# The residual scaled ahead of eight accumulating transfers, and one set of weights split earlier, in a one-core transformer layer

## The reference, cut to what matters

```
x = layer_norm(ALPHA * x + mixed, ln1_g, ln1_b)
h = square(relu(x @ w_up))                     # 512 x 4096
x = layer_norm(ALPHA * x + h @ w_down, ln2_g, ln2_b)
```

## Time and profile before

| | |
|---|---|
| three executions | 833.61, 830.8, 833.26 us; median 833.26 |
| the profiled execution | 841.54 us, its span 839.7 us, mean granted clock 0.984 |
| PE busy | 804.4 us, 96% of the span |
| DVE busy | 551.4 us, 66% |
| ACT busy | 403.2 us, 48% |
| POOL busy | 117.9 us, 14% |
| DMA | 168.45 MB, mean 201 GB/s |

### The profile page before, as it was taken

One profiled execution on the slowest core, in us unless ns is written; L12 is line 12 of the kernel. 1 busy time (PEld: TensorE's weight loads), 2 busy tenths in 40 slices (PEclk: granted clock), 3 DMA queues, 4 the chain that ended last, 5 costly groups with the idle time before them and its releaser, 6 DMA issues.

```text
span 839.7 us, 11669 instructions
## 1 busy us (share of the span) xinstructions
PE 804.4 (96%) x4779; PEld 714.0 (85%) x4779; DVE 551.4 (66%) x587; ACT 403.2 (48%) x457; POOL 117.9 (14%) x123
## 2 busy tenths in 40 slices
PE   9999999999999999999999999909999999999995
PEld 8889888898888889989988898807998899889974
DVE  4656556665569338686685777609568946974798
ACT  5658334583236225434461237601467357635843
POOL 1211111421111111111011111121012000000006
PEclk9999999999999999999999999968999999999999
DMA  9696776768676987956987497868999955555522
GB/s 312 222 306 214 188 143 145 175 125 164 202 260 165 261 176 138 310 75 171 350 281 172 59 260 190 178 109 262 280 256 265 252 202 182 172 201 198 201 101 100
DMA packets 81251, 168.45 MB, mean 201 GB/s; under 512 B 3341, under 2 KB 33078, under 8 KB 77622
## 3 DMA queue, kind: packets, MB, share of 16 engines
q1 hardware_dynamic: 58358, 109.08, 37.8%
q0 software_dynamic: 22848, 58.73, 34.4%
HBM read 165.70 MB, written 60.82 MB: 270 GB/s over the span
## 4 chain that ended last, share of the span: by engine, by line
issue 54%; PE 30%; POOL 10%; DVE 4%; DMA 1%; ACT 0%; SPq 0%; DVEq 0%; POOLq 0%
PE bank L1949 10%; PE bank L1950 10%; PE bank L1951 10%; POOL kept L697 7%; POOL kept L687 2%; DVE two L1786 1%; DVE w_lo L1221 1%; POOL y_lo L704 1%; DMA two<-in_mem_dram 1%; DVE y_lo L1221 0%; PE bank L1976 0%; POOL two L734 0%; DVE decay L1792 0%; DVE smx L1792 0%; POOL y_hi L702 0%
## 5 line engine op out<-in xcount | busy, mean ns | idle before, releaser
L1949 PE MATMUL bank<-x_hi,w_hi 128*128 128x512 f32 (+1 forms) x624 | 211.8, 339 | 0.0
L1950 PE MATMUL bank<-x_lo,w_hi 128*128 128x512 f32 (+1 forms) x624 | 210.6, 338 | 0.0
L1951 PE MATMUL bank<-x_hi,w_lo 128*128 128x512 f32 (+1 forms) x624 | 210.6, 338 | 0.0
L1949 PE MATMUL bank<-w_hi,y_hi 128*128 128x512 f32 x304 | 120.1, 395 | 25.7 <-DVE two L1786 22.7
L1221 DVE TENSOR_TENSOR w_lo<-raw,w_hi 128x2048 fp32r<-128x2048 f32 (+2 forms) x52 | 111.2, 2140 | 37.8 <-ACT w_hi L1050 28.7
L1949 PEld LDWEIGHTS bank<-x_hi,w_hi 128*128 128x128 f32 x624 | 118.4, 190 | 12.7 <-issue 0.3
L1951 PEld LDWEIGHTS bank<-x_hi,w_lo 128*128 128x128 f32 x624 | 118.4, 190 | 12.5
L1950 PEld LDWEIGHTS bank<-x_lo,w_hi 128*128 128x128 f32 x624 | 118.4, 190 | 12.2
L1951 PE MATMUL bank<-w_hi,y_lo 128*128 128x512 f32 x304 | 119.3, 392 | 0.0
L1950 PE MATMUL bank<-w_lo,y_hi 128*128 128x512 f32 x304 | 119.3, 392 | 0.0
L697 POOL DMA_DIRECT2D kept<-kept x56 | 64.6, 1153 | 361.3 <-issue 331.4
(11 more groups left out here) (269 smaller groups left out, 1388.1 us busy)
## 6 DMA issues: line engine op xcount, KB each, us to landing
kept<-kept POOLq DMA_DIRECT2D x56, 512.0 KB, 7.6
raw<-in_w_in_dram SPq DMA_DIRECT2D x22, 1024.0 KB, 7.5
raw<-kept SPq DMA_DIRECT2D x20, 1024.0 KB, 4.9
kept<-in_w_down_dram POOLq DMA_DIRECT2D x16, 1024.0 KB, 6.1
kept<-in_w_up_dram POOLq DMA_DIRECT2D x12, 1024.0 KB, 5.9
raw<-in_w_up_dram SPq DMA_DIRECT2D x9, 1024.0 KB, 7.5
gate_a<-kept SPq DMA_DIRECT2D x8, 1024.0 KB, 6.3
raw<-in_w_down_dram SPq DMA_DIRECT2D x7, 1024.0 KB, 7.2
```

Of the source, the lines that this page charges most:

```text
L1949: pe.matmul(dst, a[0], b[0], start=first, stop=False, skip_group_check=goes_on)
L1950: pe.matmul(dst, a[0], b[1], start=False, stop=False, skip_group_check=goes_on)
L1951: return pe.matmul(dst, a[1], b[0], start=False, stop=last, skip_group_check=goes_on)
```

## The change

Three edits.

1. On GpSimd: of jobs 4 and 5, only steps 0 and 1 (8 accumulating transfers) come before the scaling of the residual; steps 2 and 3 (8 more) come behind it.
2. In the last group, down m4's block is loaded during the up products, between up m3 and up m2, and split there, not into `w_hi` and `w_lo` but into the first halves of `x_hi` and `x_lo`, which nobody reads after the last up m1 (`aside`, `mlp_weights`). Its load takes a turn in the rotation of the raw buffers, so that up m2 and all behind it use the next buffer (`split_at`). down m4's form is split as soon as h22 is squared, into the place of x1's form m5 (`form_parts`).
3. On DVE in `last_rows`, m7's weights and form are split first, and the statistics of m2's rows come behind additions.

```
...
+def aside(n):
+
+    return n == down_slab(G_MLP - 1, "m4")
+
+
+def split_at(n):
+
+    at = up_slab(G_MLP - 1, "m2")
+    return at if aside(n) else n if n < at else n + 1
...
+def first_forms(g):
+    return ("m1", "m2") if g == 0 else ("m2", "m1") if g < G_MLP - 1 else ("m2", "m1", "m4")
...
         def mlp_raw(n):
-            return raw[:, n % 3, :] if n % 3 < 2 else gate_a
+            return raw[:, split_at(n) % 3, :] if split_at(n) % 3 < 2 else gate_a
...
+        def mlp_weights(n):
+            return (aside_hi, aside_lo) if aside(n) else (w_hi[:, n % 3, :], w_lo[:, n % 3, :])
+
+        def form_parts(g, name):
+
+            if g == G_MLP - 1 and name == "m4":
+                return x1_form_hi[:, X1_SLOT["m5"], :], x1_form_lo[:, X1_SLOT["m5"], :]
+            return form_hi[:, FORM_OF[name], :], form_lo[:, FORM_OF[name], :]
...
                     for name in PRODUCTS:
                         product_load("up", g, name)
-                for name in ROWS:
+                        if g == G_MLP - 1 and name == "m3":
+                            product_load("down", g, "m4")
+                for name in ROWS[0:6 if g == G_MLP - 1 else 7]:
...
-            for jobs in ((2, 3), (4, 5)):
-                begin_sums(jobs)
-                make_sums(jobs, range(4))
+            begin_sums((2, 3))
+            make_sums((2, 3), range(4))
+            begin_sums((4, 5))
+            make_sums((4, 5), (0, 1))
 
             for b in range(TB):
                 pool.wait_ge(aux_done, LNT.done("x%d1" % b))
                 pool.tensor_scalar(resid[:, b, :], resid[:, b, :], ALPHA, 1.0, ALU.mult, ALU.mult)\
                     .then_inc(resid_ready, 1)
 
+            make_sums((4, 5), (2, 3))
             begin_sums((6,))
             make_sums((6,), range(4))
...
-                if n == 2:
+                if aside(n):
+                    act.wait_ge(mlp_done, slab_done(up_slab(G_MLP - 1, "m1"), 1))
+                elif n == 2:
                     act.wait_ge(tile_done, mlp_round(0) * MAIN)
                 elif n > 2:
-                    act.wait_ge(mlp_done, slab_over(n - 3))
+                    act.wait_ge(mlp_done, slab_done(n - 3, 1))
...
                 mlp_hi(up_slab(g, "m3"))
+                if g == G_MLP - 1:
+                    mlp_hi(down_slab(g, "m4"))
                 copied("m5", h22, 1.0)
...
-                activated(h22)
+                mark(activated(h22))
+                if g == G_MLP - 1:
+                    marked()
+                    form_to_hi(g, "m4")
...
                 mlp_lo(up_slab(g, "m3"))
+                if g == G_MLP - 1:
+                    mlp_lo(down_slab(g, "m4"))
                 mlp_lo(up_slab(g, "m2"))
...
                 mlp_lo(down_slab(g, "m2"))
+                if g == G_MLP - 1:
+                    form_to_lo(g, "m4")
...
-                complete("m2", 0)
-                complete("m2", 1)
                 mlp_lo(down_slab(g, "m7"))
+                form_to_lo(g, "m7")
+                down_add(g, "m2", 0)
+                down_add(g, "m2", 1)
                 down_add(g, "m6", 0)
+                half_stats(g, "m2", 0)
                 complete("m3", 0)
                 moments(0, 2)
-                form_to_lo(g, "m7")
                 scales(0)
-                form_to_lo(g, "m4")
                 down_add(g, "m6", 1)
-                mlp_lo(down_slab(g, "m4"))
+                half_stats(g, "m2", 1)
                 dve.wait_ge(ln_landed, 64)
...
```

More of the change, by code:

```diff
@@ L139, in up_added_of, with in_order @@
     return 6 * (g - 1) + 2 * UP_ADDS.index(name) + p + 1
+def first_forms(g):
+    return ("m1", "m2") if g == 0 else ("m2", "m1") if g < G_MLP - 1 else ("m2", "m1", "m4")
+def in_order(g, names, name):
+    return 7 * g + (first_forms(g) + tuple(n for n in names if n not in first_forms(g))).index(name) + 1
 def form_rounded(g, name):
-    return 7 * g + ((("m2", "m1") if g else ("m1", "m2")) + ("m5", "m7", "m6", "m3", "m4")).index(name) + 1
+    return in_order(g, ("m5", "m7", "m6", "m3", "m4"), name)
 def form_ready(g, name):
-    return 7 * g + ((("m2", "m1") if g else ("m1", "m2")) + ("m5", "m6", "m3", "m7", "m4")).index(name) + 1
+    return in_order(g, ("m5", "m6", "m3", "m7", "m4"), name)
 def made(g, name, r):
@@ L330, in build @@
         X1_SLOT = dict(m5=0, m7=1, m6=2, m3=3)
+        aside_hi, aside_lo = (t[:, 0:PAIRS, :].rearrange("p k c -> p (k c)") for t in (x_hi, x_lo))
         h11, h12, h22 = two[:, 4, :], two[:, 5, :], small[:, 8192:9216]
@@ L603, in mlp_load @@
             def mlp_load(n, src, k):
-                if n < 2:
-                    sp.wait_ge(slab_lo, S_MLP - 2 + n + 1)
-                elif n == 2:
+                at = split_at(n)
+                if at < 2:
+                    sp.wait_ge(slab_lo, S_MLP - 2 + at + 1)
+                elif at == 2:
                     sp.wait_ge(tile_done, mlp_round(0) * MAIN)
                 else:
-                    sp.wait_ge(slab_lo, S_MLP + n - 3 + 1)
+                    sp.wait_ge(slab_lo, S_MLP + at - 3 + 1)
                 to = mlp_raw(n).rearrange("p (k c) -> p k c", k=k)
-                sp.dma_start(to, src).then_inc(third_landed if n % 3 == 2 else slab_landed[n % 3], 16)
+                sp.dma_start(to, src).then_inc(third_landed if at % 3 == 2 else slab_landed[at % 3], 16)
             def product_load(kind, g, name):
@@ L1043, in mlp_hi @@
             def mlp_hi(n):
-                if n == 2:
+                if aside(n):
+                    act.wait_ge(mlp_done, slab_done(up_slab(G_MLP - 1, "m1"), 1))
+                elif n == 2:
                     act.wait_ge(tile_done, mlp_round(0) * MAIN)
                 elif n > 2:
-                    act.wait_ge(mlp_done, slab_over(n - 3))
+                    act.wait_ge(mlp_done, slab_done(n - 3, 1))
                 mlp_landed(act, n)
-                act.activation(w_hi[:, n % 3, :], mlp_raw(n), ACT.Copy).then_inc(slab_hi, 1)
+                act.activation(mlp_weights(n)[0], mlp_raw(n), ACT.Copy).then_inc(slab_hi, 1)
             def x1_parts(b):
@@ L1083, in form_to_hi @@
             def form_to_hi(g, name):
-                act.activation(form_hi[:, FORM_OF[name], :], h_of[name], ACT.Copy).then_inc(forms_hi, 1)
+                act.activation(form_parts(g, name)[0], h_of[name], ACT.Copy).then_inc(forms_hi, 1)
             def made_to_hi(g, name):
@@ L1682, in mlp_lo @@
             def mlp_lo(n):
-                dve.wait_ge(slab_hi, S_MLP + n + 1)
-                low_of(w_lo[:, n % 3, :], mlp_raw(n), w_hi[:, n % 3, :]).then_inc(slab_lo, 1)
+                dve.wait_ge(slab_hi, S_MLP + split_at(n) + 1)
+                high, low = mlp_weights(n)
+                low_of(low, mlp_raw(n), high).then_inc(slab_lo, 1)
             def mixed(b, e):
@@ L2384, in row @@
                 n = down_slab(g, name)
-                slab(S_MLP + n)
+                slab(S_MLP + split_at(n))
+                high, low = mlp_weights(n)
                 pe.wait_ge(forms_ready, form_ready(g, name))
@@ L2390, in row @@
                     mm = three(bank[down_bank(g, name) + r],
-                               both(form_hi, form_lo, ALL, FORM_OF[name], slice(j * 256 + r * P, j * 256 + (r + 1) * P)),
-                               w_part(n % 3, j * WID, WID), opens and j == 0, j == PAIRS - 1, not opens)
+                               tuple(f[:, j * 256 + r * P:j * 256 + (r + 1) * P] for f in form_parts(g, name)),
+                               (high[:, j * WID:(j + 1) * WID], low[:, j * WID:(j + 1) * WID]), opens and j == 0, j == PAIRS - 1, not opens)
                 mm.then_inc(mlp_done, 1)
```

21 lines of the change are left out of this document (9 added, 12 removed).

## The result

| | before | after |
|---|---|---|
| executions timed together | 832.57 us median, 830.8 to 833.61, 4 | 814.11 us median, 813.35 to 814.51, 4 |
| ratio | | 0.9779, 95% interval 0.9759 to 0.98 |
| span of the profiled execution | 839.7 us | 812.6 us |
| the profiled execution itself | 841.54 us | 814.37 us |
| mean granted clock in it | 0.984 | 0.997 |

The kernel is faster by 2.2%, 18.5 us by these medians. 814.11 lies 6.1 us above the forecast and 0.11 above the upper end of the range. The sum made against the profiled execution was 812.2; the profiled execution of the changed kernel took 814.37.

The account below looks back on a forecast made before the run. TensorE was taken to bound the kernel, busy 804.4 of 839.7 us with one 22.7 us pause. Gains of 25.6 (pause) and 3.7 (tail) sum to 29.3; between 812.2 and 804.0 it forecast 808 us, range 802.5 to 814.

Parts of the forecast that it names:

- The sum made against the profiled execution: Whole kernel: 25.6 us from the pause plus 3.7 from the tail, 29.3 off 841.54, giving 812.2 us.
- I take the middle, 808: Whole kernel: midway between 812.2 (the 8.3 us lie in the pause) and 804.0 us (they lie elsewhere).
- the first case: The forecast itself, chance 0.55: the plain runs' 8.3 us lie in the pause or elsewhere, upper bound 812.2 us.
- Groups 1 and 2 run the same order without a pause, so I charge nothing: Group 0 behind the removed pause: DVE's later splits cost PE no new wait, 0 us.
- DVE must follow ... 3.7: Last group's tail: DVE, counted in its new order, ends earlier with PE; gain 3.7 us, bounds 0 to 3.8.
- Sharing with DVE: Scaling beside DVE's x1 forms: delays DVE by 0 to 4.2 us, covered by 8.7 us; taken as zero.
- if PE stood right behind it: At the x1 forms: with DVE paying the full 4.2 us for the shared port, the sum would be 4.2 smaller.
- The plain runs have the whole pause: Rival on the plain runs: the 8.3 us lie outside the pause, the full 29.3 us comes off, 804.0; chance 0.20.
- Packed transfers: Rival at 545 to 569: loads meet GpSimd's transfers, one lands late, PE loses 5.4 and 2.5 us, 816; chance 0.12.
- The tail gives nothing: Rival in the last group: DVE or GpSimd's last blocks hold the end, 811.7 us; chance 0.09.
- The sync queue blocked by m4's load: Rival: down m4's load waits for job 6 in the in-order queue, slower than before from 86 us late; chance 0.02.
- The pause stays: Rival at group 0's first down addition: something other than the residual holds it, 830 us; chance 0.02.

Follow-up runs that it names:

- experiment 1: The kernel before, unchanged, run and profiled again: 841.01 us median in five executions, the profiled one 834.24 us.
- experiment 10: The kernel before, unchanged, run a third time for its scatter: 830.81 us median in ten executions.
- experiment 9: The changed kernel without GpSimd's multiplication by ln2_g for the last of its five half blocks: 812.68 us median.
- experiment 3: The kernel before with only the scaling moved ahead of eight transfers, the last group as before: 817.39 us median, ratio 0.9831.
- experiment 2: The changed kernel, unaltered, run again in the same batch as the scaling-only kernel: 813.58 us median.
- experiment 6: The changed kernel with twelve instead of eight of the sixteen transfers ahead of the scaling: 815.76 us median, ratio 0.9784.
- experiment 8: The changed kernel without steps 2 and 3 of jobs 4 and 5, eight accumulating transfers left out: 813.48 us median.
- experiment 7: The kernel with only the scaling moved, plus m7's weights and form split first in the last rows, m4 still split there: 816.61 us median.
- experiment 5: The changed kernel with fourteen instead of eight of the sixteen transfers ahead of the scaling: 819.54 us median.

## Why the prediction was right or wrong, point by point

**The direction and the mechanism were right.** One pause, made by the order of GpSimd's list and not by its work, held most of the gain; it went whole, no new wait of its size took its place, and the clock stayed up. Against the profiled execution the sum was 29.3 us and the spans differ by 27.1.

**The step that failed is "I take the middle, 808".** The prediction saw that the 8.3 us between the profiled execution and the median could lie in the pause or elsewhere, argued that the chain of transfers made the pause the likelier place, and then took half of each. Experiments 1 and 10 put all of it in the pause: from the first profile to that of experiment 1, execution, chain and pause move together by 7.3, 7.35 and 7.2 us, to that of experiment 10 by 8.8, 8.4 and 9.2. With that, the sum gives 812.2, which I had as the upper bound of the first case and not as its value. This is 4.2 of the 6.1 us by which the forecast missed. The argument was there to be finished. A pause whose length is set by a chain that nothing else waits for scatters by itself, and a profile is one draw from it: the earlier trace rows showed one of the longest, 22.7 us, where the median of all 60 executions on record is 833.5 us, which goes with a pause near 15.

**The range was also too narrow at its upper end**, since it took the sum against the profile as exact. The other 1.9 us of the miss lie here. Three terms of the sum were mis-sized:
- "Groups 1 and 2 run the same order without a pause, so I charge nothing": group 0's DVE is 1.4 us later in the order than group 1's (m7's weights split 1.0 us ahead of ACT's mark behind m6 instead of 2.4), and PE loses 0.51 us at m4's row 0. The pause had hidden that. Another 0.2 lie in PE itself: from 563.42 m4's 24 matmuls take 5.65 us where a product takes 5.44, two of the steps being 0.31 and 0.29 instead of 0.23; why, no run shows. Together they are the 0.7 of the second line.
- "DVE must follow ... 3.7": 3.82 to the last addition, but the end behind it grew by 0.63, most of it through three stores at once (experiment 9). Net 3.2 between the traces; 3.8 between the medians of experiments 3 and 2, where the clock may have its part. I had followed DVE and PE to the end; GpSimd's last blocks stand in the prediction only as a rival that takes the whole gain, with no term for a part of it.
- The start: 0.97 us more before 545 in this execution, and -0.9 to +0.8 in the other profiles. In this execution all of it is there by 472.7, when neither the scaling nor anything else of the change has begun (the same matmul started at 472.73 and, before, at 471.75). It is scatter that the sum has no term for.

**Sharing with DVE** was bounded rightly: 0 to 4.2 us on DVE, 3.4 measured, covered. The rule of the Trainium skill ("SBUF — State Buffer", the shared GPSIMD/Vector port) agrees with the trace here: two-input DVE operations and GpSimd's scaling took 8.0 and 8.4 us together where 4.6 and 4.4 were their times alone. Its cost for PE was nothing in this place, and over 1 us in that of experiment 6, which is the case the prediction described as "if PE stood right behind it".

**The rivals.** *The plain runs have the whole pause* (804.0): refuted, and so is the use I made there of the Trainium skill ("TensorE: Matmul & The Clock Gate", on the back-to-back issue gap). The page gives that formula for the isolated matmul and not for a stream of weight loads and matmuls, which PE's work is here. PE's pace is the same in all profiles, 101.45 us for the same eighteen roundings, and none of the 8.3 us lay in it. *Packed transfers*: they packed (DMA share 1.00), in the changed kernel one load held ACT up by 0.5 us, and PE lost nothing by it (the spread told under experiment 8). *The tail gives nothing*: refuted by 3.2 to 3.8 us; its grain of truth is GpSimd's last half. *The sync queue blocked by m4's load*: the load was issued at 724.99 (723 was the estimate) and job 6's last transfer at 661.13, so the cover was 56 us once its landing, a median 7.8 us, is taken off. *The pause stays*: no.

## What to carry to other kernels

When an engine's order puts a short step that others need behind a long chain that nobody needs soon, moving the step can be worth the whole pause plus the clock's recovery, as here; put it where neither engine that shares with it is the one waited for next, and leave room for the chain's scatter (eight transfers ahead had 35 us by the forecast and 26 in the latest chain that was profiled, in experiment 7, fourteen had too little). Before carrying a sum from a profile to a median, ask whether the removed wait is itself what scatters: if so, the difference between the two belongs to the wait, not half of it. After a pause is gone, follow the engine it had let catch up, and the last output of every engine, down to the stores.

## What the runs showed of the hardware that I had not expected

- GpSimd's chain of transfers scatters by some 20 us. Its eighth accumulating transfer of jobs 4 and 5, up to which all the kernels here are the same on GpSimd, was issued between 481.13 (experiment 9) and 506.52 us (experiment 7) in the twelve profiles. The executions of the kernel before took 821.5 to 842.4 us, and in its three profiles one wait holds the difference to within 0.5 us. PE's work over 100 us repeats to 0.01 us.
- Four scalings by GpSimd beside DVE's two-input operations took 6.2 to 9.6 us instead of 4.4, and the DVE operations up to 1.7 times their time.
- The last three stores of 256 KB took 2.1, 2.4 and 2.6 us to land when they were issued within 0.8 us, against 2.0, 2.0 and 2.1 with 1.6 and 0.7 us between them. Distance is not all of it: two stores issued 0.4 us apart took 2.5 and 3.1 us in the changed kernel and 2.1 and 2.3 in the kernel before.
- The clock fell behind short gaps of PE in some executions and not in others: behind a gap of 2.12 us the granted clock was 0.50 for 3.4 us (experiment 5), behind gaps of 1.13 and 1.80 it was 0.66 over 5 us in experiment 3 and 1.00 in the kernel before, and behind one of 2.77 it was 1.00 (experiment 7).
